# Prompt attention of a one-core decoder layer: the two heads of an output tile take turns, and values are weighed per query tile

## The chip, the core and the metric

The kernel runs on one core of a Trainium2 chip. The metric is the device time of one execution in microseconds (us). The engines are TensorE (PE, with its weight loads listed apart as PEld), VectorE (DVE), ScalarE (ACT), GpSimd (POOL) and SyncE (SP, which issues most DMAs). A name like L1465 is a line of the kernel file.

## What is computed

One layer over 512 prompt tokens and 8 sample tokens: a half-step feed-forward block, a mixer with 8 forgetting-attention heads (FoX) and 8 native-sparse-attention heads (NSA), and a second half-step feed-forward block. The change is in the mixer's attention over the prompt alone, cut here to that:

```python
# FoX, per head h, 64 dims, causal, 512 queries in blocks of 128
s = q @ k.T * scale + cum[q] - cum[k];  s = where(kpos <= qpos, s, NEG)
o_fox = softmax(s) @ v
# NSA, per head h (key/value head h // 4): selected and window branches, the same shape each
o = gate_slc * softmax(mask(q @ k_slc.T)) @ v_slc + gate_win * softmax(mask(q @ k_win.T)) @ v_win + compressed branch
```

With 512 tokens every block is selected and the window covers everything, so both NSA branches are plain causal attention.

## The kernel before, in words

The prompt's queries are cut into four tiles of 128 (i = 0 to 3); tile i looks at the keys 0 to 128(i+1). A unit is one head, one branch and one query tile. There are 96: 32 for FoX (8 heads by 4 tiles) and 64 for NSA (8 heads by 2 branches by 4 tiles). `unit(v)` (L128) numbers them: head by head, and inside a head (and branch) the tiles i = 0, 1, 2, 3. Four units with the same head and branch are a run; there are 24 runs.

A unit passes five steps, spread over the engines:

- `scores(v)` on TensorE (L1426): two matmuls of query against key (width 256, 256, 384, 512 for i = 0 to 3), for FoX one bf16 matmul with the forget sums (L1440), and one with the causal mask (L1442), all into a PSUM bank, of which FoX has four and NSA three.
- VectorE takes the row maximum (L1051), ScalarE the exponential with its sum (L756), VectorE the reciprocal (L1056). The scaling (L448) is on VectorE for i = 2 and 3 and on GpSimd for i = 0 and 1.
- `turn_p(w)` on TensorE (L1445): i+1 transposes of 128 by 128 (L1451) into PSUM bank 4 or 5.
- `turn_out` (L458) copies them to the buffer PTS (L464): VectorE for even units, ScalarE for odd ones.
- `weigh` on TensorE (L1455): the values VT times PTS, f32, into 64 of the 128 PSUM partitions of bank 6 or 7: partitions 0 to 63 for the even head of a tile of the output, 64 to 127 for the odd head. Before, one call `weigh(run, kb)` does a whole run's key block kb: one matmul, whose moving side is the queries from kb*128 to 512, so 512, 384, 256 and 128 columns for kb = 0 to 3.

Two heads make one output tile OT; `pair_out` (L744, ScalarE) copies a finished one out of PSUM (L746), and the next user of that bank waits for it. There are 8.

The order on each engine is written out by hand. In TensorE's `attention` (L1485) a step v issues scores(v), then turn_p(v-3), then from v = 8 after the stage's start one weigh of the list, so one key block at each step; what is left is issued at the end in a row. In NSA, from unit 52 to 83, each step also issues two matmuls of the compression windows (`windows`, L1471, L1479). ScalarE and VectorE each have a loop over the same v, with exp(v) and then the copy of v-3, and max(v), reciprocal and scale of v-1, and the copy of v-3.

An f32 matmul of the program shows as two records in the trace, each with a weight load of its own: the 96 calls of weigh are 192 records of L1465.

FoX attention stands between two parts of the input projection (L1308); NSA attention follows the second part. After NSA, SP waits for the last weigh before it loads more of the sample tokens' caches (L555), and GpSimd before it clears buffers (L1279).

Of the kernel before, what the change touches and what calls it, by code (L numbers as in the profile page):

```python
# [24 lines left out]
F32 = mybir.dt.float32  # L25
# [7 lines left out]
P = 128  # L33
D_MODEL, SEQ, DEC, PAST, PAGE = 1024, 512, 8, 256, 128
TOK = SEQ + DEC
HALF = TOK // 2
DH, HF, HN, HKV = 64, 8, 8, 2
# [5 lines left out]
QT = SEQ // P  # L43
# [81 lines left out]
    return sum(t in kinds for t in TILES[:j])  # L125


def unit(v):  # L128

    if v < 4 * HF:  # L130
        return True, v // 4, 0, v % 4, v // 4
    w = v - 4 * HF
    return False, w // 8, (w // 4) % 2, w % 4, HF + w // 4


def runs_of_pair(t):

    return range(2 * t, 2 * t + 2) if t < 4 else range(HF + 4 * (t - 4), HF + 4 * (t - 3))


class Step:
# [24 lines left out]
def layer_kernel(nc, I, O):  # L166
    with ExitStack() as ctx:
        made = {}

        def sem(name):  # L170
            if name not in made:
                made[name] = ctx.enter_context(nc.semaphore(name))
            return made[name]
# [78 lines left out]
        att = Region(a0, asize)  # L252
# [5 lines left out]
        v0 = att.at  # L258
        VT = att.put("VT", [P, QT, 512], F32)
        p0 = att.at  # L260
        PTS = att.put("PTS", [P, 2, QT, SEQ], F32)
        t0 = att.at
        TR = att.put("TR", [P, 4, TOK], F32)
        r0 = att.at
# [192 lines left out]

        def turn_out(eng, copy, w, name):  # L458

            _, _, _, i, run = unit(w)  # L460
            eng.wait_ge(sem("att_turned"), w + 1)
            if run >= 2:
                eng.wait_ge(sem("att_pv"), run - 1)
            copy(PTS[:, run % 2, 0:i + 1, P * i:P * i + P],  # L464
                 ps[:, 4 + w % 2, 0:P * (i + 1)].rearrange("p (a n) -> p a n", n=P)).then_inc(sem(name), 1)

        block = ctx.enter_context(nc.Block())
# [3 lines left out]
        def _(sp):  # L471
# [79 lines left out]
            for g in range(NPAGE):  # L551
                sp.dma_start(VF[g // 8][:, g % 8, :],
                             I["fox_v"][bass.ds(page[g], 1)].rearrange("a p n -> p (a n)")
                             ).then_inc(sem("vf_in"), 16)
            sp.wait_ge(sem("att_pv"), HF + 2 * HN)  # L555
            for name in sorted({stored_sem(j) for j in STORED}):
                sp.wait_ge(sem(name), max(stored_count(j) for j in STORED if stored_sem(j) == name))
            for g in range(NPAGE):
# [30 lines left out]
        def _(act):  # L589
# [152 lines left out]


            def pair_out(t):  # L744
                act.wait_ge(sem("att_pv"), runs_of_pair(t)[-1] + 1)
                nc.scalar.copy(OT[:, t, 0:SEQ], ps[:, 6 + t % 2, :]).then_inc(sem("att_out"), 1)  # L746

            def attention(u0, u1, pairs):
                pairs = list(pairs)
                for v in range(u0, u1 + 3):  # L750
                    if v < u1:
                        W = P * (unit(v)[3] + 1)
                        act.wait_ge(sem("att_max"), v + 1)
                        if v >= 4:
                            act.wait_ge(sem("att_turned"), v - 3)
                        nc.scalar.activation(PR[:, v % 4, 0:W], ps[:, score_bank(v), 0:W], ACT.Exp,  # L756
                                             bias=row_max[:, v:v + 1], accum_out=row_sum[:, v:v + 1]).then_inc(
                            sem("att_exp"), 1)
                    w = v - 3
                    if w >= u0 and w % 2:  # L760
                        turn_out(act, nc.scalar.copy, w, "att_odd_out")
                    if pairs and w > 4 * runs_of_pair(pairs[0])[-1] + 6:
                        pair_out(pairs.pop(0))
                for t in pairs:
                    pair_out(t)
# [456 lines left out]
        def _(pool):  # L1222
# [53 lines left out]
            nc.gpsimd.memset(QBN[:, :], 0.0).then_inc(sem("qb_cleared"), 1)  # L1276
            attention(4 * HF, 96)

            pool.wait_ge(sem("att_pv"), HF + 2 * HN)  # L1279
            nc.gpsimd.memset(KCS[:, :, :].bitcast(F32), 0.0).then_inc(sem("kc_cleared"), 1)  # L1280
            nc.gpsimd.memset(VCZ[:, :, :], 0.0).then_inc(sem("vc_cleared"), 1)
            nc.gpsimd.memset(PZ[0][:, :, :], 0.0).then_inc(sem("pz_cleared0"), 1)
# [12 lines left out]
        def _(pe):  # L1295
# [156 lines left out]
                                            PR[:, w % 4, kb * P:kb * P + P], ident)  # L1452
                q.then_inc(sem("att_turned"), 1)

            def weigh(run, kb):  # L1455

                fox, h, br, _, _ = unit(4 * run)
                t, j = (h // 2) + (0 if fox else 4), h % 2
                c = h * DH if fox else br * P + (h // 4) * DH
                if kb == 0:  # L1460
                    pe.wait_ge(sem("att_even_out"), 2 * run + 2)
                    pe.wait_ge(sem("att_odd_out"), 2 * run + 2)
                    if t >= 2 and j == 0 and br == 0:
                        pe.wait_ge(sem("att_out"), t - 1)
                q = nc.tensor.matmul(ps[64 * j:64 * j + 64, 6 + t % 2, kb * P:SEQ], VT[:, kb, c:c + DH],  # L1465
                                     PTS[:, run % 2, kb, kb * P:SEQ], start=kb == 0 and br == 0,
                                     stop=kb == QT - 1 and (fox or br == 1), skip_group_check=True)
                if kb == QT - 1:
                    q.then_inc(sem("att_pv"), 1)

            def windows(step):  # L1471

# [10 lines left out]
                        q.then_inc(sem("cmp_hid"), 1)  # L1483

            def attention(u0, u1):  # L1485
                parts = [(run, kb) for run in range(u0 // 4, u1 // 4) for kb in range(QT)]
                for v in range(u0, u1 + 3):
                    if v < u1:
                        scores(v)
                    if v - 3 >= u0:  # L1490
                        turn_p(v - 3)
                    if v >= 4 * parts[0][0] + 8:
                        weigh(*parts.pop(0))
                    if HID_FROM <= v < HID_FROM + 2 * CMP_LEN // HID_PER_UNIT:
                        windows(v - HID_FROM)
                for run, kb in parts:
                    weigh(run, kb)

            project(0, NB1)
            pe.wait_ge(sem("stack_lo"), of_kind(NB1, STACKED))  # L1500
# [275 lines left out]
```

## Time and profile before

| | |
|---|---|
| median of 3 runs | 1329.59 us (1329.27 to 1329.98) |
| span of the profiled execution | 1327.7 us |
| TensorE busy | 1259.9 us, 95% |
| VectorE, ScalarE, GpSimd busy | 569.3, 454.3, 174.6 us |
| FoX attention in the profile | about 507 to 563 us |
| NSA attention in the profile | about 631 to 768 us |

The profile is one execution. Its span, 1327.7 us, lies 1.9 us below the median of the timed runs; that much lies around the span. A row of a timeline gives start, duration, engine, line, operation, output<-input, the tile of the array (rows by columns), and how many records were merged. In brackets stands the engine's idle time before it and what ended it. Ends of matmuls are modelled and overlap, so the time from one start to the next says what an operation really takes, not its duration.

### The profile page before, as it was taken

What the parts mean: (1) busy time and instruction counts of PE and PEld (TensorE: products, weight loads), DVE (VectorE), ACT (ScalarE), POOL (GpSimd) and SP (SyncE); (2) the same over time, 40 slices, a digit from 0 to 9 for tenths busy, and PEclk for the clock granted to TensorE, in tenths of its full rate; (3) what the DMA queues carried; (4) which work ended last, traced back from release to release, by engine and by line L of the source; (5) the groups of instructions that cost most, each with busy time, mean ns of one, the idle gap of its engine ahead of it and who ended that gap; (6) DMA issues with size and microseconds to landing.
All of it is one profiled execution on the core that took longest, in us unless ns stands there. A gap on an engine that the chain in (4) does not pass through costs nothing.

```text
span 1327.7 us, 22995 instructions
## 1 busy us (share of the span) xinstructions
PE 1259.9 (95%) x9234; PEld 1121.9 (85%) x9234; DVE 569.3 (43%) x896; ACT 454.3 (34%) x767; POOL 174.6 (13%) x157
## 2 busy tenths in 40 slices
PE   8999999999998898999999988798999999999994
PEld 6999999999996895499566543596999999999993
DVE  4334333343337665456533542636433333343333
ACT  5222212222335635442533432345322221222342
POOL 0111100101114001122101100034011100001113
PEclk9999999999999999999999989899999999999997
DMA  6222233222231241011600544011122222322221
GB/s 254 96 95 95 72 96 111 80 88 83 80 123 41 74 144 48 1 64 65 211 0 0 193 117 137 32 65 64 64 95 95 79 87 95 109 79 92 80 80 65
DMA packets 46001, 117.91 MB, mean 89 GB/s; under 512 B 4154, under 2 KB 21818, under 8 KB 39874
## 3 DMA queue, kind: packets, MB, share of 16 engines
q1 hardware_dynamic: 42738, 110.95, 24.8%
q10 hardware_dynamic: 3184, 5.88, 1.2%
q8 instruction: 54, 0.88, 0.3%
q14 instruction: 25, 0.20, 0.0%
HBM read 110.93 MB, written 7.97 MB: 90 GB/s over the span
## 4 chain that ended last, share of the span: by engine, by line
PE 87%; DVE 5%; ACT 3%; issue 2%; DMA 1%; POOL 1%; POOLq 0%; ACTq 0%; SPq 0%; DVEq 0%
PE ps L1308 68%; PE ps L1465 5%; PE ps L1479 3%; PE ps L1436 3%; PE ps L1451 2%; DVE UT L890 1%; PE ps L1317 1%; PE ps L1599 1%; DVE XL L870 1%; POOL H L1252 1%; DVE QST L964 1%; ACT QST L674 1%; PE ps L1608 1%; DMA RAW<-in_w_gu 0%; PE ps L1401 0%
## 5 line engine op out<-in xcount | busy, mean ns | idle before, releaser
L1308 PE MATMUL ps<-XH,WH 128*128 128x260 f32 x1904 | 390.6, 286 | 20.0 <-DVE XL L870 13.7
L1308 PE MATMUL ps<-XH,WL 128*128 128x260 f32 x1904 | 384.6, 284 | 0.0
L1308 PE MATMUL ps<-XL,WH 128*128 128x260 f32 x1904 | 384.2, 283 | 0.0
L403 ACT CAST WH<-RAW 128x1024 fp32r<-128x1024 f32 (+2 forms) x183 | 174.8, 956 | 505.1 <-PE ps L1308 495.8
L1308 PEld LDWEIGHTS ps<-XH,WH 128*128 128x128 f32 x1904 | 295.7, 189 | 27.6 <-DVE XL L870 14.0
L1308 PEld LDWEIGHTS ps<-XH,WL 128*128 128x128 f32 x1904 | 294.5, 189 | 0.0
L1308 PEld LDWEIGHTS ps<-XL,WH 128*128 128x128 f32 x1904 | 294.0, 189 | 0.0
L406 DVE TENSOR_TENSOR WL<-RAW,WH 128x1024 fp32r<-128x1024 f32 (+2 forms) x183 | 203.5, 1112 | 154.8 <-ACT WH L403 153.6
L1308 PE MATMUL ps<-UL,WH 128*128 128x260 f32 x704 | 141.9, 283 | 0.0
L1308 PE MATMUL ps<-UH,WL 128*128 128x260 f32 x704 | 141.5, 282 | 0.0
L1308 PE MATMUL ps<-UH,WH 128*128 128x260 f32 x704 | 141.4, 282 | 0.0
L1242 POOL TENSOR_TENSOR UL<-HT,UH 128x520 f32 (+1 forms) x44 | 57.6, 1310 | 612.3 <-ACT UH L641 612.3
L1308 PEld LDWEIGHTS ps<-UH,WL 128*128 128x128 f32 x704 | 108.5, 188 | 0.0
L1308 PEld LDWEIGHTS ps<-UH,WH 128*128 128x128 f32 x704 | 108.4, 188 | 0.0
L1308 PEld LDWEIGHTS ps<-UL,WH 128*128 128x128 f32 x704 | 108.3, 188 | 0.0
L906 DVE TENSOR_TENSOR UT<-ps,token_rstd 128x520 f32<-128x520 f32 x44 | 30.8, 700 | 145.8 <-PE ps L1308 145.8
L1051 DVE TENSOR_REDUCE row_max<-ps 128x1 f32<-128x128 f32 (+1 forms) x96 | 46.9, 489 | 91.4 <-PE ps L1442 91.4
L902 DVE TENSOR_TENSOR GT<-ps,token_rstd 128x520 f32<-128x520 f32 x44 | 30.8, 699 | 128.2 <-PE ps L1308 119.8
L756 ACT ACTIVATE PR<-ps,row_max 128x128 f32<-128x128 f32 (+1 forms) x96 | 50.6, 527 | 95.7 <-DVE row_max L1051 95.0
L1465 PE MATMUL ps<-PTS,VT 128*64 128x512 f32 (+1 forms) x192 | 70.4, 456 | 0.0
L1436 PE MATMUL ps<-KST,QST 128*128 128x256 f32 (+1 forms) x192 | 61.4, 404 | 2.3 <-ACT v_new L709 1.0
L1436 PEld LDWEIGHTS ps<-KST,QST 128*128 128x128 f32 x192 | 33.1, 199 | 30.6 <-ACT PR L756 17.3
(229 smaller groups left out, 1056.5 us busy)
## 6 DMA issues: line engine op xcount, KB each, us to landing
RAW<-in_w_gu SPq DMA_DIRECT2D x44, 1024.0 KB, 4.8
RAW<-in_w_down SPq DMA_DIRECT2D x16, 768.0 KB, 4.6
RAW<-in_w_in SPq DMA_DIRECT2D x11, 1024.0 KB, 4.8
RAW<-in_w_down SPq DMA_DIRECT2D x16, 640.0 KB, 4.3
KF<-in_fox_k SPq DMA_DIRECT2D x16, 256.0 KB, 4.1
VF<-in_fox_v SPq DMA_DIRECT2D x16, 256.0 KB, 5.8
RAW<-in_w_out SPq DMA_DIRECT2D x4, 1024.0 KB, 5.0
H<-in_x SPq DMA_DIRECT2D x4, 520.0 KB, 7.4
```

What stands on the lines that cost most here:

```text
L403: nc.scalar.copy(WH[:, par, 0:width], RAW[:, slot, j, 0:width]).then_inc(w_hi, 1)
L406: nc.vector.tensor_tensor(WL[:, par, 0:width], RAW[:, slot, j, 0:width], WH[:, par, 0:width], ALU.subtract).then_inc(w_lo, 1)
L756: nc.scalar.activation(PR[:, v % 4, 0:W], ps[:, score_bank(v), 0:W], ACT.Exp, bias=row_max[:, v:v + 1], accum_out=row_sum[:, v:v + 1]).the ...
L902: nc.vector.tensor_tensor(two(GT[:, st.par, :]), halves(0), two(R1[:, :]), ALU.mult).then_inc(sem("evac"), 1)
L906: nc.vector.tensor_tensor(two(UT[:, st.par, :]), halves(1), two(R1[:, :]), ALU.mult).then_inc(sem("evac"), 1)
L1051: nc.vector.reduce_max(row_max[:, v:v + 1], ps[:, score_bank(v), 0:W], AX.X, negate=True).then_inc(sem("att_max"), 1)
L1242: nc.gpsimd.tensor_tensor(row(UL, st.m), HT[:, st.par, :], row(UH, st.m), ALU.subtract).then_inc(sem("hid_lo"), 1)
L1308: q = nc.tensor.matmul(ps[:, 2 * slot + half, 0:HALF], w[:, par, cols], x[:, kt0 + kt, half * HALF:(half + 1) * HALF], start=first and kt ...
L1436: nc.tensor.matmul(bank[:, 0:n], QST[:, h, part, i * P:i * P + P], KST[:, k, 0:n], start=part == 0, stop=False, skip_group_check=True)
L1451: q = nc.tensor.transpose(ps[:, 4 + w % 2, kb * P:kb * P + P], PR[:, w % 4, kb * P:kb * P + P], ident)
L1465: q = nc.tensor.matmul(ps[64 * j:64 * j + 64, 6 + t % 2, kb * P:SEQ], VT[:, kb, c:c + DH], PTS[:, run % 2, kb, kb * P:SEQ], start=kb == 0 ...
L1479: q = nc.tensor.matmul(ps[:, 3, 0:N_WIN], W1[n][:, j, :], view(X[n][:, :], j, [[CMP_STRIDE, N_WIN]]), start=j == 0, stop=j == CMP_LEN - 1)
```

## The change

- `unit(v)` counts differently: the two heads of an output tile alternate, so units come as tile 0 of both heads, tile 1 of both, and so on. In NSA branch follows branch as before, but inside a pair of heads.
- `weigh(n)` is called once for two units (every second step, at v - 6 = 2n) and does one query tile of both heads: for each key block kb up to i, head even and head odd one after the other, each 128 columns wide, into partitions 0 to 63 and 64 to 127 of the same bank.
- PTS becomes eight slots of one unit each, in place of two slots of one run each. The copies wait for `att_pv` per pair of units.
- `pair_out`, the waits of SP and GpSimd and the threshold in ScalarE's loop count pairs of units (48) in place of runs (24).

```diff
+PAIRS = 48
+PT_SLOTS = 8
 def unit(v):
     if v < 4 * HF:
-        return True, v // 4, 0, v % 4, v // 4
+        return True, 2 * (v // 8) + v % 2, 0, v // 2 % 4, v // 8
     w = v - 4 * HF
-    return False, w // 8, (w // 4) % 2, w % 4, HF + w // 4
+    return False, 2 * (w // 16) + w % 2, w // 8 % 2, w // 2 % 4, 4 + w // 16
-def runs_of_pair(t):
-    return range(2 * t, 2 * t + 2) if t < 4 else range(HF + 4 * (t - 4), HF + 4 * (t - 3))
+def pairs_until(t):
+    return 4 * (t + 1) if t < 4 else 16 + 8 * (t - 3)
...
-        PTS = att.put("PTS", [P, 2, QT, SEQ], F32)
+        PTS = att.put("PTS", [P, PT_SLOTS, QT, P], F32)
...
-            if run >= 2:
-                eng.wait_ge(sem("att_pv"), run - 1)
-            copy(PTS[:, run % 2, 0:i + 1, P * i:P * i + P],
+            if w >= PT_SLOTS:
+                eng.wait_ge(sem("att_pv"), (w - PT_SLOTS) // 2 + 1)
+            copy(PTS[:, w % PT_SLOTS, 0:i + 1, :],
...
-            def weigh(run, kb):
-                ...
-                q = nc.tensor.matmul(ps[64 * j:64 * j + 64, 6 + t % 2, kb * P:SEQ], VT[:, kb, c:c + DH],
-                                     PTS[:, run % 2, kb, kb * P:SEQ], start=kb == 0 and br == 0, ...)
+            def weigh(n):
+                pe.wait_ge(sem("att_even_out"), n + 1)
+                pe.wait_ge(sem("att_odd_out"), n + 1)
+                fox, _, br, i, t = unit(2 * n)
+                first = br == 0 and i == 0
+                if first and t >= 2:
+                    pe.wait_ge(sem("att_out"), t - 1)
+                for kb in range(i + 1):
+                    for j in (0, 1):
+                        h = unit(2 * n + j)[1]
+                        c = h * DH if fox else br * P + (h // 4) * DH
+                        q = nc.tensor.matmul(ps[64 * j:64 * j + 64, 6 + t % 2, i * P:i * P + P], VT[:, kb, c:c + DH],
+                                             PTS[:, (2 * n + j) % PT_SLOTS, kb, :], start=first and kb == 0, ...)
+                q.then_inc(sem("att_pv"), 1)
...
-                    if v >= 4 * parts[0][0] + 8:
-                        weigh(*parts.pop(0))
+                    if v % 2 == 0 and v - 6 >= u0:
+                        weigh((v - 6) // 2)
...
-                for run, kb in parts:
-                    weigh(run, kb)
+                weigh(u1 // 2 - 1)
```

## Rows read from the trace of the kernel before

**Rows 1.** The page: TensorE's share, and VectorE's, of the whole span.
```profile
PE 1259.9 (95%) x9234; PEld 1121.9 (85%) x9234; DVE 569.3 (43%) x896; ACT 454.3 (34%) x767; POOL 174.6 (13%) x157
```

**Rows 2.** The chain that ended last, 505 to 775 us, shares by line.
```profile
by line: PE ps L1465 23.9%; PE ps L1308 21.6%; PE ps L1479 15.1%; PE ps L1436 14.5%; PE ps L1451 9.9%; PE ps L1401 2.3%; issue 2.2%; PE ps L1442 2.2%; PE ps L1440 1.9%; DVE row_max L1051 1.0%; DVE VCZ L1097 0.6%; ACT L782 0.5%; ACT VT L707 
```

**Rows 3.** Busy time of each engine in one run of FoX, NSA, NSA with windows.
```profile
536.47:543.23 6.76, 6.76 (x36) 3.45 (x35) 3.73 (x13) 3.21 (x10) 1.53 (x2) 1.00 0.01 2
646.13:652.34 6.21, 6.21 (x31) 3.10 (x32) 3.87 (x13) 3.21 (x10) 1.00 (x2) 1.00 0.94 271
680.20:690.70 10.50, 10.50 (x47) 6.39 (x47) 3.91 (x13) 3.21 (x10) 1.00 (x2) 1.00 0.00 0
```

**Rows 4.** TensorE's timeline, FoX steps each with a weigh.
```profile
540.63 0.22 PE L1442 MATMUL ps<-causalb,identb 128*128 128x128 bf16 x1
540.68 0.61 PE L1451 MATMUL ps<-consts,PR 128*128 128x128 f32 x4
541.22 0.65 PE L1465 MATMUL ps<-PTS,VT 128*64 128x256 f32 x2
541.80 0.73 PE L1436 MATMUL ps<-KST,QST 128*128 128x512 f32 x2
...
542.65 0.28 PE L1451 MATMUL ps<-consts,PR 128*128 128x128 f32 x1
542.87 0.43 PE L1465 MATMUL ps<-PTS,VT 128*64 128x128 f32 x2
543.23 0.39 PE L1436 MATMUL ps<-KST,QST 128*128 128x256 f32 x1
```

**Rows 5.** The same timeline at the start of FoX, before the first weigh.
```profile
514.30 0.63 PE L1451 MATMUL ps<-consts,PR 128*128 128x128 f32 x4
514.68 0.71 PE L1436 MATMUL ps<-KST,QST 128*128 128x512 f32 x2
...
515.51 0.28 PE L1451 MATMUL ps<-consts,PR 128*128 128x128 f32 x1
515.55 0.48 PE L1436 MATMUL ps<-KST,QST 128*128 128x256 f32 x2
```

**Rows 6.** The weigh matmuls by form, 510 to 775 us: count, busy us, mean ns.
```profile
L1465 PE MATMUL ps<-PTS,VT 128*64 128x512 f32 x48 | 25.7, 617 | 0.0
L1465 PE MATMUL ps<-PTS,VT 128*64 128x128 f32 x48 | 10.2, 294 | 0.0
```

**Rows 7.** Sample tokens: 32 records, 128 columns, half array, back to back (chain; line L1608).
```profile
832.08 3.64 PE ps L1608 x32
...
L1608 PEld LDWEIGHTS ps<-VS,PZS x32: 133/137/138, 832.0 to 835.3; 128*64 128x64 f32 x32
L1608 PE MATMUL ps<-VS,PZS x32: 272/273/323, 832.0 to 835.4; 128*64 128x128 f32 x32
```

**Rows 8.** Timeline: two weight loads of one weigh; f32r matmuls of the projection.
```profile
541.22 0.19 PEld L1465 LDWEIGHTS ps<-PTS,VT 128*64 128x64 f32 x2 [0.17 <-issue]
...
612.21 0.40 PE L1308 MATMUL ps<-XL,WH 128*128 128x260 f32 x2
612.45 0.40 PE L1308 MATMUL ps<-XH,WL 128*128 128x260 f32 x2
```

**Rows 9.** VectorE by form, 510 to 775 us: maximum, reciprocal, scale and copy.
```profile
L1051 DVE TENSOR_REDUCE row_max<-ps 128x1 f32<-128x512 f32 x24 | 16.6, 691 | 33.7 <-PE ps L1442 33.7
L1056 DVE RECIPROCAL row_inv<-row_sum 128x1 f32<-128x1 f32 x95 | 14.6, 154 | 1.2 <-ACT PR L756 1.0
L1051 DVE TENSOR_REDUCE row_max<-ps 128x1 f32<-128x384 f32 x24 | 13.3, 555 | 26.1 <-PE ps L1442 26.1
L464 DVE COPY PTS<-ps 128x384 f32<-128x384 f32 x24 | 12.9, 539 | 0.0
...
L448 DVE TENSOR_SCALAR PR<-PR,row_inv,gates 128x512 f32<-128x512 f32 x16 | 8.7, 547 | 0.6
L448 DVE TENSOR_SCALAR PR<-PR,row_inv,gates 128x384 f32<-128x384 f32 x16 | 7.7, 479 | 0.6
...
L464 DVE COPY PTS<-ps 128x128 f32<-128x128 f32 x24 | 6.8, 283 | 0.0
L1051 DVE TENSOR_REDUCE row_max<-ps 128x1 f32<-128x128 f32 x23 | 6.5, 284 | 8.4 <-PE ps L1442 8.4
```

**Rows 10.** Timeline at the end of FoX.
```profile
559.96 3.17 PE L1465 MATMUL ps<-PTS,VT 128*64 128x256 f32 x12
560.07 0.58 ACT L464 COPY PTS<-ps 128x512 f32<-128x512 f32 x1 [1.70 <-PE ps L1451]
```

**Rows 11.** SP's issues of the window data, and the first matmuls that use them.
```profile
639.43 0.43 SPq L539 DMA_DIRECT2D XK<-out_nsa  x1
...
L1479 PE MATMUL ps<-XK,W1K x64: 449/450/522, 660.2 to 700.3; 128*128 128x161 f32 x64
```

More of the change, by code:

```diff
@@ L458, in turn_out @@
         def turn_out(eng, copy, w, name):
-            _, _, _, i, run = unit(w)
+            i = unit(w)[3]
             eng.wait_ge(sem("att_turned"), w + 1)
-            if run >= 2:
-                eng.wait_ge(sem("att_pv"), run - 1)
-            copy(PTS[:, run % 2, 0:i + 1, P * i:P * i + P],
+            if w >= PT_SLOTS:
+                eng.wait_ge(sem("att_pv"), (w - PT_SLOTS) // 2 + 1)
+            copy(PTS[:, w % PT_SLOTS, 0:i + 1, :],
                  ps[:, 4 + w % 2, 0:P * (i + 1)].rearrange("p (a n) -> p a n", n=P)).then_inc(sem(name), 1)
@@ L554, in _ @@
                              ).then_inc(sem("vf_in"), 16)
-            sp.wait_ge(sem("att_pv"), HF + 2 * HN)
+            sp.wait_ge(sem("att_pv"), PAIRS)
             for name in sorted({stored_sem(j) for j in STORED}):
@@ L744, in pair_out @@
             def pair_out(t):
-                act.wait_ge(sem("att_pv"), runs_of_pair(t)[-1] + 1)
+                act.wait_ge(sem("att_pv"), pairs_until(t))
                 nc.scalar.copy(OT[:, t, 0:SEQ], ps[:, 6 + t % 2, :]).then_inc(sem("att_out"), 1)
@@ L761, in attention @@
                         turn_out(act, nc.scalar.copy, w, "att_odd_out")
-                    if pairs and w > 4 * runs_of_pair(pairs[0])[-1] + 6:
+                    if pairs and w > 2 * pairs_until(pairs[0]) + 2:
                         pair_out(pairs.pop(0))
@@ L1277, in _ @@
             attention(4 * HF, 96)
-            pool.wait_ge(sem("att_pv"), HF + 2 * HN)
+            pool.wait_ge(sem("att_pv"), PAIRS)
             nc.gpsimd.memset(KCS[:, :, :].bitcast(F32), 0.0).then_inc(sem("kc_cleared"), 1)
@@ L1453, in turn_p @@
                 q.then_inc(sem("att_turned"), 1)
-            def weigh(run, kb):
[L1457 to L1464, printed above, removed]
-                q = nc.tensor.matmul(ps[64 * j:64 * j + 64, 6 + t % 2, kb * P:SEQ], VT[:, kb, c:c + DH],
[L1466 to L1469, printed above, removed]
+            def weigh(n):
[10 more added lines that the diff above has]
+                        q = nc.tensor.matmul(ps[64 * j:64 * j + 64, 6 + t % 2, i * P:i * P + P], VT[:, kb, c:c + DH],
+                                             PTS[:, (2 * n + j) % PT_SLOTS, kb, :], start=first and kb == 0,
+                                             stop=i == QT - 1 and kb == i and (fox or br == 1),
+                                             skip_group_check=True)
+                q.then_inc(sem("att_pv"), 1)
             def windows(step):
@@ L1485, in attention @@
             def attention(u0, u1):
-                parts = [(run, kb) for run in range(u0 // 4, u1 // 4) for kb in range(QT)]
                 for v in range(u0, u1 + 3):
```

## The prediction

> **What bounds the kernel now.** I read the page first: TensorE is busy for 95% of the span, VectorE for 43% [rows 1]. The chain of waits for the stretch of both attentions says the same in detail: almost all of its pieces are TensorE's, and the largest line is the weighing of the values, L1465, with 23.9% of 270 us, 64.5 us [rows 2]. The busy times of single runs show that no engine but TensorE is full: in a FoX run of four units TensorE works all of 6.76 us, VectorE 3.73, ScalarE 3.21, GpSimd 1.53; in an NSA run 6.21 against 3.87, 3.21 and 1.00; in an NSA run with the compression windows 10.50 against 3.91. The granted clock is 1.00 in all three, the level of 2.4 GHz [rows 3]. So whatever TensorE is spared here comes off the span, until VectorE is next.
>
> **What the weighing costs now.** Two records of 128 columns in a row without a change of form start 0.114 us apart (32 records in 3.64 us) [rows 7]; an f32 record takes two clocks a column (128 columns are 0.107 us at 2.4 GHz, the other 0.007 is the price of a short record). A run has 1280 columns in two records each, so 2560 times 2 clocks, 2.13 us; 24 runs take 51.2 us. (The means of the forms, 617 ns for 512 columns and 294 for 128, are longer, since ends are modelled and overlap [rows 6].) That leaves 13 of the chain's 64.5 us for something else. The timeline shows what. All other matmuls around it use the whole array (128*128), the weighing uses half the columns (128*64). From one transpose to the next scores it is 0.04 us with no weigh between [rows 5] and 0.58 us with one of 128 columns [rows 4]: 0.58 - 0.04 - 0.213 = 0.33 us more than its columns. With four transposes and 256 columns it is 1.12 against 0.38: 1.12 - 0.38 - 0.427 = 0.31 us. I take 0.32 us for going into the half-array form and out again.
>
> A rule of the Trainium skill bears on that: TensorEngine Tiling (Array Packing), section Tiling Modes, says that changing the tiling mode, not just the tile, drains the engine. The 0.31 and 0.33 us are this case's number for it.
>
> **Fewer blocks.** Before, each step from v = 8 has a weigh, 27 in FoX and 59 in NSA with the left-over ones in one block, 86 blocks. After, every second step has one: steps 6 to 34 in FoX, 15 blocks (the last two calls adjoin), and 31 in NSA, 46 blocks. 40 blocks fewer at 0.32 us: 12.8 us saved.
>
> **The matmuls themselves.** The columns stay: 10 matmuls of 128 columns per head and branch in place of 4 of up to 512, so 24 times 10, 240 matmuls, 480 records. If they run one after the other as in rows 7, they take 480 x 0.114 = 54.7 us, 3.5 us more than now (the records of 512 columns pay hardly any short-record price: the 12 left-over records with 1664 columns need 2.77 us of columns and are 3.17 long to their modelled end [rows 10]).
>
> But each pair now names two different halves of the array. No row of the trace before has matmuls of both halves side by side (at the end of FoX the other half waits for a copy), so this is unknown and I bound it. Upper end: no overlap, 54.7 us. Lower end: all overlap, 27.4 us. Which is nearer? A half-array record uses 64 columns; the other 64 stand idle. What could forbid a second record beside it are the shared paths. The load path doesn't: two loads of 64 columns take 0.19 us where one takes 0.135, so they are 0.055 us apart [rows 8], 480 of them 26.4 us. The moving side doesn't seem to: the projection's f32r records stream 260 columns in 0.12 us [rows 8], twice what an f32 record asks for. And loads of the same rows already go on beside a running matmul: loads of 0.137 us at a spacing of 0.114 [rows 7]. So I take overlap as the likelier case. The order is even, even, odd, odd in records (each matmul is two), and starts stay in order; then the second record of one half goes beside the first of the other, and a block of r records takes r/2 + 1 places rather than r/2. Eight units have four blocks, of 4, 8, 12 and 16 records, so 3 + 5 + 7 + 9 = 24 places in place of 40. Twelve such groups: 288 places at 0.114 us, 32.8 us. Against 51.2 us that saves 18.4 us.
>
> Statements of the Trainium skill speak to this, and the sum uses none. TensorEngine Tiling (Array Packing), sections Tiling Modes and Theoretical Speedup, says that different tiles can run loads and matmuls in parallel, with up to twice the throughput at 64 columns; by it the weighing would take about 27 us. The Trainium skill's TensorE: Matmul & The Clock Gate, Part 3, gives 2.38 times for three column tiles, but also says that a load overlaps a running matmul only when the row groups differ, and here both halves use all rows. By that last rule every load would be exposed, 480 x 0.055 = 26 us more; rows 7 speak against it, since their loads overlap.
>
> **What comes next once TensorE is faster.** With these savings eight units take 13.5 - 1.28 - 1.54 = 10.7 us in FoX, 12.4 - 2.8 = 9.6 in NSA and 18.2 with windows. VectorE has 7.5 us and 7.7 us of work for eight units [rows 3], plus 0.26: its copies are now of 128, 256, 384 and 512 columns in place of 128 and 384 twice (by rows 9 the step per 128 columns is 0.13 us, so 0.41 and 0.67 us for the two not shown). On average it has room. But the heavy units now come in fours (tiles 2, 2, 3, 3), all scaled by VectorE. I walked through that stretch by its order: from the scores of the second tile-2 unit until the last tile-3 unit may be turned VectorE has four maxima (384, 512, 512 and 128 columns: 0.56, 0.69, 0.69, 0.28), four reciprocals (0.62), four scales (twice 0.48, twice 0.55) and two copies (0.41, 0.54), 5.8 us [rows 9]. TensorE has in between five transposing calls (14 transposes of 0.107, 1.5 us), the scores of five units (two records of 256 to 512 columns at one clock a column and the mask: 1.8 us in NSA; with the forget sums 2.4 in FoX), two weighs of 3 and 5 places (0.9 us) with 0.64 for their forms, and 0.07 to 0.1 us a step besides (the step from 514.68 to 515.55 [rows 5] is that much longer than its columns): 5.3 us in NSA and 5.9 in FoX. So about 0.5 us of waiting per group in NSA without windows (units 32 to 51 and 84 to 95, four groups), 2 us, none in FoX and none under the windows. The bounds: 0, and 12 us, if a wait of 1.5 us comes in each of the eight groups without windows (then VectorE's chain, not TensorE, sets them).
>
> GpSimd's scales come in fours too, 3.1 us in FoX at most for eight units (twice 1.53 [rows 3]) out of 10.7; hidden. The waits added: copies wait for the weigh of eight units before, issued five steps earlier, hidden; the weigh waits for two copies made two steps earlier, hidden; if it were not, the next scores would be queued behind it. The window data land far ahead of need: the last is issued at 639.4, used first at 660.2 [rows 11], and that use moves forward by some 6 us. The ends of both stages: the last pair's heaviest units follow each other, so the last scale is late while TensorE has only one weigh left to cover it (before, five left-over ones followed): 0.5 us each, 1 us. At the starts the weighing begins two steps earlier, in a stretch with waits: no price.
>
> **The sum.** -12.8 - 18.4 + 2 + 1 = -28.2 us. The profiled execution goes from 1327.7 to 1299.5 us, and with the 1.9 us around it to 1301.4 us. The range of this case: 1293 (full overlap, no waits: -12.8 - 23.8) to 1311 (12 us of waits in place of 2).
>
> **The rivals.** First: the halves don't overlap; only the switches go. -12.8 + 3.5 = -9.3, 1320.3 us. For it: nothing in the trace has ever run two halves at once, and one sequencer feeds both in order. Against it: the arguments of the paths above. Its range is 1316 to 1326.
>
> Second: they overlap, but VectorE's chain sets both attentions outside the windows, and the gain there is lost for the most part; -12.8 - 18.4 + 15, 1313.4 us. Against it: 83% load at most.
>
> Third, the slower one: a change from one half to the other costs a drain as the change of form does. There are 1 + 3 + 5 + 7 = 16 such changes in a group, 192 in all. Half of 0.32 us each makes 30.7 us, so 1329.6 - 9.3 + 30.7 = 1351 us. It decides from 0.049 us per change on. For it: a change of form does drain (rows 4 and 5). Against it: the form stays 128*64, and the output partitions differ, so there is nothing to wait for.
>
> Fourth: the price of 0.32 us belongs to each matmul group's length or to the wait for copies, and isn't spared: then 0 to 3 us are lost or won, about 1330 us. For it, little: rows 4 and 5 differ in the weigh alone.
>
> **Chances.** Forecast (overlap, TensorE still the bound) 0.58; first rival 0.26; second 0.06; third 0.06; fourth 0.04. A measurement of this kernel tells 0.2%, 2.7 us, from no change. Faster: 0.58 + 0.26 + 0.06 = 0.90; same 0.04; slower 0.06. The range for 8 in 10 has to take in the first rival's centre and most of its spread and the forecast's: 1292 to 1325 us; above it lie the third and fourth and a little of the first, below it what a better start of the stages might add.
>
> **What would show it.** In the profile after: 480 records of L1465, all 128 columns; their starts in a block of 16 records some 0.06 us apart if they overlap, 0.11 if not, 0.2 or more if a change of half drains. A weigh's entry and exit still about 0.32 us, at half as many places. VectorE's waits before its maxima shrink from the 33.7 us shown for the widest form [rows 9]; TensorE would show waits for the scale (L448) ahead of transposes in NSA outside the windows, about 2 us. The FoX stage shrinks by about 10 us, NSA by 18. The prediction is wrong if the pairs are serial, if loads of the other half wait for the running matmul, or if TensorE waits for VectorE for more than some 5 us.

## The result

The changed kernel takes 1296.09 us (median of 4 runs, 1294.54 to 1297.29) against 1329.78 us before (1329.27 to 1330.54): ratio 0.9747, interval 0.9733 to 0.9761, 33.7 us less. The forecast was 1301.4 us, with 1292 to 1325 as its range.

The page of the changed kernel: the span, each engine's busy time (to set against [rows 1]), and the granted clock in 40 slices. The last line is the clock of the kernel before.

```profile
span 1293.2 us, 23595 instructions
...
PE 1226.7 (95%) x9522; PEld 1130.8 (87%) x9522; DVE 572.3 (44%) x896; ACT 451.6 (35%) x767; POOL 174.9 (14%) x157
...
PEclk9999999999998999999999999898999999999997
```

```profile
PEclk9999999999999999999999989899999999999997
```

TensorE is as full as before, with 288 records more and 33.2 us less of busy time; the others do what they did. The weighing by form, in the window of both attentions (count, busy us, mean ns), answers to [rows 6]; the chain's shares by line there answer to [rows 2].

```profile
L1471 PE MATMUL ps<-PTS,VT 128*64 128x128 f32 x480 | 36.7, 283 | 0.0
```

```profile
by line: PE ps L1312 25.3%; PE ps L1485 16.4%; PE ps L1440 14.1%; PE ps L1471 13.8%; PE ps L1455 11.4%; issue 3.9%; PE ps L1405 2.7%; PE ps L1446 2.6%; DVE row_max L1055 2.5%; PE ps L1444 2.1%; DVE PTS L468 0.9%; ACT PTS L468 0.6%; ACT L786
```

The weighing (now L1471) held 64.5 us of the chain before and holds 13.8% of 230 us, 32 us, now: 33 us are gone in this one line. Read from the starts of TensorE's first and last matmuls of each stage, FoX took 56.2 us and takes 44.1; the projection between takes 68.9 both times; NSA took 135.0 and takes 112.2; the rest of the kernel after it 560.0 and 560.6.

TensorE's timeline shows the blocks. A row's count is of records, two for each matmul; the start of the next row tells what a block really takes. FoX (first four rows) answers to [rows 4]; the last pairs are NSA under the windows.

```profile
531.17 1.09 PE L1471 MATMUL ps<-PTS,VT 128*64 128x128 f32 x16
532.20 0.62 PE L1440 MATMUL ps<-KST,QST 128*128 128x384 f32 x2
...
534.18 0.44 PE L1471 MATMUL ps<-PTS,VT 128*64 128x128 f32 x4
534.55 0.73 PE L1440 MATMUL ps<-KST,QST 128*128 128x512 f32 x2
...
669.62 0.66 PE L1471 MATMUL ps<-PTS,VT 128*64 128x128 f32 x8
670.21 1.34 PE L1485 MATMUL ps<-XK,W1K 128*128 128x161 f32 x4
...
674.07 0.88 PE L1471 MATMUL ps<-PTS,VT 128*64 128x128 f32 x12
674.88 1.34 PE L1485 MATMUL ps<-XK,W1K 128*128 128x161 f32 x4
```

Blocks of 4, 8, 12 and 16 records take 0.37, 0.59, 0.81 and 1.03 us to the next instruction: 0.0545 us a record and 0.15 us beside. About 0.05 us of the 0.15 lies between the first two starts of each half (0.16 us in place of 0.109), the rest at the way out of the form. That is half of what a record costs in [rows 7]: two halves of the array work side by side, without the one place that I had given up in each block. The records' own starts say the same: they come in pairs, one for each half, 6 ns apart, and after the first step each half starts a new one every 0.109 us. Two rows of the view of busy time in short stretches, of L1471 alone (length, busy, number of records running, granted clock), show two records from the first moment on.

```profile
541.44:541.60 0.16, 0.15 (x2) 1.00 0.00 0
541.60:541.71 0.11, 0.11 (x4) 1.00 0.00 0
```

### The profile page after: what moved, and what is told of

Same layout as the page of the kernel before. It is cut to its first block, busy times and chain, and to the rows that moved or that the text cites. A ratio compares the mean times of both kernels' runs of the same rounds, so it can differ in the third digit from the quotient of the medians.

```text
span 1293.2 us, 23595 instructions
## 1 busy us (share of the span) xinstructions
PE 1226.7 (95%) x9522; PEld 1130.8 (87%) x9522; DVE 572.3 (44%) x896; ACT 451.6 (35%) x767; POOL 174.9 (14%) x157
## 4 chain that ended last, share of the span: by engine, by line
PE 86%; DVE 6%; ACT 4%; issue 2%; DMA 1%; POOL 1%; POOLq 0%; ACTq 0%; SPq 0%; DVEq 0%
PE ps L1312 70%; PE ps L1485 3%; PE ps L1440 3%; PE ps L1471 2%; PE ps L1455 2%; PE ps L1321 1%; DVE UT L894 1%; PE ps L1603 1%; DVE XL L874 1%; POOL H L1256 1%; DVE QST L968 1%; ACT QST L678 1%; PE ps L1612 1%; PE ps L1405 0%; PE ps L1446 0%
## 5 line engine op out<-in xcount | busy, mean ns | idle before, releaser
L1246 POOL TENSOR_TENSOR UL<-HT,UH 128x520 f32 (+1 forms) x44 | 57.9, 1315 | 612.0 <-ACT UH L645 612.0
L760 ACT ACTIVATE PR<-ps,row_max 128x128 f32<-128x128 f32 (+3 forms) x96 | 50.7, 529 | 72.9 <-DVE row_max L1055 72.3
L1055 DVE TENSOR_REDUCE row_max<-ps 128x1 f32<-128x128 f32 (+3 forms) x96 | 46.8, 488 | 58.9 <-PE ps L1446 58.7
L1440 PE MATMUL ps<-KST,QST 128*128 128x256 f32 (+2 forms) x192 | 61.9, 408 | 2.0 <-ACT v_new L713 1.0
L645 ACT CAST UH<-HT 128x520 f32 (+1 forms) x44 | 27.6, 627 | 86.0 <-DVE HT L917 86.0
L1455 PE MATMUL ps<-consts,PR 128*128 128x128 f32 x240 | 43.6, 280 | 3.3 <-ACT PTS L468 2.9
```

Of the source, the lines that this page charges most:

```text
L645: nc.scalar.copy(row(UH, st.m), HT[:, st.par, :]).then_inc(sem("hid_hi"), 1)
L1055: nc.vector.reduce_max(row_max[:, v:v + 1], ps[:, score_bank(v), 0:W], AX.X, negate=True).then_inc(sem("att_max"), 1)
L1246: nc.gpsimd.tensor_tensor(row(UL, st.m), HT[:, st.par, :], row(UH, st.m), ALU.subtract).then_inc(sem("hid_lo"), 1)
L1440: nc.tensor.matmul(bank[:, 0:n], QST[:, h, part, i * P:i * P + P], KST[:, k, 0:n], start=part == 0, stop=False, skip_group_check=True)
L1455: q = nc.tensor.transpose(ps[:, 4 + w % 2, kb * P:kb * P + P], PR[:, w % 4, kb * P:kb * P + P], ident)
```

## The experiments

Times are medians; before is 1329.1 to 1329.3 us in these comparisons, and the changed kernel in its own run among them 1295.02 us. Where several numbers of one stage stand together, they are read from the same starts as above. The spread between executions of one kernel goes in part with the mean granted clock: the kernel with one half for both heads takes 1311.25 and 1311.4 us at 0.977, and 1308.6 and 1309.2 us at 0.979. The single steps of 1 to 3 us further down (two pairs, the copy first, the scale on GpSimd, and the last two together) have intervals that overlap the changed kernel's, 0.973 to 0.9756; that of two pairs with the copy first ends where the changed kernel's begins. One half, the heads in turn, one unit, the narrow matmuls and all three stand clear of it.

**One half for both heads.** In NSA both heads write one half.

```diff
-                        q = nc.tensor.matmul(ps[64 * j:64 * j + 64, ...
+                        half = j if fox else br
+                        q = nc.tensor.matmul(ps[64 * half:64 * half + 64, ...
...
```

> The changed kernel, but in the NSA stage both heads of a block write the same column half (partitions 0 to 63 in the first branch, 64 to 127 in the second), so the two heads' sums are mixed there; blocks, records (480 in all, 320 of them here) and order stay. Theory: the halves overlap, 0.055 us a record in pairs of halves against 0.114 in one half, so 320 x 0.059 = 18.9 us come back, less some 3 us of waits for copies that then vanish: 1312 to 1315 us. Rival: the gain is that of fewer changes of form and the halves add nothing: 1296 us, as the changed kernel.

Measured: 1310.22 us, ratio to before 0.9851 (0.9834 to 0.9867), 14.1 to 15.2 us slower than the changed kernel. FoX, which is not touched, takes 44.0 us as there; NSA takes 127.8 in place of 112.2. NSA blocks of the trace:

```profile
633.80 1.96 PE L1472 MATMUL ps<-PTS,VT 128*64 128x128 f32 x16
635.69 0.62 PE L1440 MATMUL ps<-KST,QST 128*128 128x384 f32 x2
...
637.30 0.65 PE L1472 MATMUL ps<-PTS,VT 128*64 128x128 f32 x4
637.88 0.73 PE L1440 MATMUL ps<-KST,QST 128*128 128x512 f32 x2
```

16 records take 1.89 us against 1.03, four take 0.58 against 0.37: 0.109 us a record with the same 0.15 beside. 320 x 0.0545 = 17.4 us; 15.6 us came back in the stage. Under the windows, where TensorE never waits, it is 7.8 us for 144 records, the full 0.0545 each; the 1.8 us that are missing all lie outside the windows, where TensorE waited before too. The rival is out: the overlap is real, and it hangs on the two heads' records naming different halves. I had 1312 to 1315 us, from 0.114 us for a record where it is 0.109.

**The heads in turn.** First all of the even head, then all of the odd.

```diff
-                for kb in range(i + 1):
-                    for j in (0, 1):
+                for j in (0, 1):
+                    for kb in range(i + 1):
```

> The changed kernel, but inside a block all key blocks of the even head come first and then all of the odd head, in place of alternating. If matmuls start strictly in the order of the program, each half runs alone, 0.114 us a record, and nearly the whole overlap is lost: 480 x 0.059 = 28 us less the one place where the halves meet in each of 48 blocks (2.6 us) and the waits that vanish: 1318 to 1322 us. Rival: TensorE holds records of both halves back and starts them out of order: 1296 us.

Measured: 1304.25 us, ratio 0.9806 (0.979 to 0.9822): neither of the two. Blocks of this trace, and then the number of records running in three successive stretches of the last of them:

```profile
640.27 0.44 PE L1471 MATMUL ps<-PTS,VT 128*64 128x128 f32 x4
640.64 0.73 PE L1440 MATMUL ps<-KST,QST 128*128 128x512 f32 x2
...
643.13 0.66 PE L1471 MATMUL ps<-PTS,VT 128*64 128x128 f32 x8
643.72 0.50 PE L1440 MATMUL ps<-KST,QST 128*128 128x256 f32 x2
...
645.52 1.15 PE L1471 MATMUL ps<-PTS,VT 128*64 128x128 f32 x12
646.60 0.50 PE L1440 MATMUL ps<-KST,QST 128*128 128x256 f32 x2
...
647.76 1.58 PE L1471 MATMUL ps<-PTS,VT 128*64 128x128 f32 x16
649.27 1.07 PE L1485 MATMUL ps<-XK,W1K 128*128 128x161 f32 x3
```

```profile
647.75:648.24 0.49, 0.48 (x4) 1.00 0.00 0
648.24:648.60 0.36, 0.36 (x9) 1.00 0.00 0
648.60:649.10 0.50, 0.50 (x10) 1.00 0.00 0
```

A block of 4 or 8 records loses nothing (0.37 and 0.59 us), one of 12 takes 1.08 in place of 0.81 and one of 16 takes 1.51 in place of 1.03. In strict order of the program the second head would begin after the first one's last record has begun, and 16 records would take about 15 x 0.109 + 0.15 = 1.8 us. In the records' starts the odd head begins 0.49 us into the block of 16, beside the fifth of the even head's eight, with three of them not begun; in the block of 12 it begins beside the third of six, again with three not begun. So in this trace TensorE went past three records that waited for their half, and no further. Per group of eight units the loss is 0.27 + 0.48 = 0.75 us, for twelve groups 9.0 us; 8.2 to 9.2 us were measured (1304.25 against 1296.09 and 1295.02).

The Trainium skill, TensorE: Matmul & The Clock Gate, Part 3, says that matmuls start and end strictly in order of the program. For records of different column halves this trace shows otherwise.

**Two and two.** Two key blocks of one head, then the same two of the other, four records each.

```diff
-                for kb in range(i + 1):
-                    for j in (0, 1):
+                for j, kb in [(j, kb) for a in range(0, i + 1, 2) for j in (0, 1) for kb in range(a, min(a + 2, i + 1))]:
```

> The changed kernel, but a block takes two key blocks of the even head, then the same two of the odd head, so four records of one half and four of the other in turn. If TensorE can begin the other half while up to three records of this half have not started (as the starts in the kernel with the heads in turn show), nothing is lost: 1296 us. If records start strictly in the order of the program, a block of 16 takes 1.4 us in place of 0.9 and the kernel some 12 us more: 1308 us.

Measured: 1296.19 us, ratio 0.9753 (0.9738 to 0.9768), against 0.9743 (0.973 to 0.9756) for the changed kernel beside it: no difference that can be told. Its blocks of 8 and 12 records take what they take in the changed kernel to within 0.01 us, and a block of 16 takes 0.05 us more, so the order costs at most 0.8 us in all. Three waiting records are passed, as read from the kernel before this one.

**The changed kernel again.**

> The changed kernel itself, run again beside the next three as their measure: 1295 to 1297 us.

Measured: 1295.02 us (1294.8 to 1297.62). It stood beside two and two (above), the copy first with the scale on GpSimd, and all three (below). Its FoX stage takes 43.4 us in the profile, where the first profile had 44.1, and the clock says why. The first row is the first profile's FoX, the second this one's; then follow, in the same order, the starts of NSA up to the first window matmul (the last columns are the granted clock, the DMA share and GB/s).

```profile
507.47:551.59 44.12, 42.86 (x369) 30.36 (x369) 30.86 (x96) 27.59 (x85) 12.15 (x16) 0.96 0.01 1
509.28:552.65 43.37, 41.30 (x364) 29.36 (x368) 30.86 (x96) 27.34 (x85) 12.08 (x16) 1.00 0.01 1
620.47:644.00 23.53, 22.45 (x185) 16.53 (x185) 17.60 (x58) 14.72 (x49) 5.71 (x12) 0.93 0.84 278
621.45:645.59 24.14, 23.51 (x185) 17.36 (x185) 17.79 (x58) 14.79 (x49) 5.69 (x12) 0.87 0.83 272
```

The granted clock of 0.96 is 3.4 us of the stage at the lower level of 1.2 GHz; without them FoX is 0.75 us shorter, and with some 3 us more of them (0.87 against 0.93) the start of NSA is 0.6 us longer. So stages of single profiles are good to about 0.7 us, and more of a claim than that rests on medians.

**One unit in a block.** The new order of units and tiles, but each head weighed at a step of its own: `weigh(m)` does unit m, one head, alone.

```diff
-                    if v % 2 == 0 and v - 6 >= u0:
-                        weigh((v - 6) // 2)
+                    if v - 6 >= u0:
+                        weigh(v - 6)
...
-                weigh(u1 // 2 - 1)
+                for m in (u1 - 3, u1 - 2, u1 - 1):
+                    weigh(m)
```

> The new order of units and the weighing per query tile, but a block at each step for one head alone (90 blocks in place of 46), so never two halves side by side. Theory: 44 more changes of form at 0.32 us, 14.1 us, and no overlap, 480 x 0.059 = 28.3 us: 1296 + 42 = 1338 us, slower than before by 8. Rival, the overlap is worth nothing: 1310 us. Rival, the change of form costs nothing: 1324 us.

Measured: 1328.41 us, ratio 0.9992 (0.9982 to 1.0001): no difference from before. So the new order and the weighing per tile bring nothing alone that shows in the medians; it is the pairing, with the overlap and 44 blocks fewer, that brings 32 to 33 us. In the stretch of the windows, where TensorE never waits, the forecast's prices hold: 82.82 us here, 68.95 in the changed kernel. Of the 13.87 us the columns account for 8.7 (152 records at 0.109 against 144 at 0.0545 in that stretch), which leaves 5.15 us for 16 blocks, 0.32 us each.

I had 42 us between this kernel and the changed one, and 33 were measured. 2 us of the miss are the 0.114 us a record for 0.109. Another 2 us are an oversight about this kernel: its last blocks of each stage adjoin, and there the two heads do meet. NSA's last block:

```profile
762.28 2.24 PE L1471 MATMUL ps<-PTS,VT 128*64 128x128 f32 x28
```

Less one record's 0.28 us, its last record starts 1.96 us after the first, where 28 records of one half would need 27 x 0.109 and 0.05, 3.0 us. In the starts, the second head begins 0.275 us into the block with three records of the first not begun. The block at the end of FoX is the same, so 2.1 us are saved in both.

That leaves 38.2 us by the prices, and the two profiles are 31.9 apart in the two stages. Most of the other 6.3 us can be read. TensorE's listed waits for scales and copies come to 8.5 us in the changed kernel (its largest rows stand under two pairs below) and to 3.9 in this one:

```profile
PEld ps L1455 <- POOL PR L452: 1.8, 5, 0.8
...
PEld ps L1471 <- ACT PTS L468: 0.8, 5, 0.2
PE ps L1455 <- POOL PR L452: 0.7, 2, 0.6
PE ps L1455 <- DVE PTS L468: 0.4, 2, 0.2
```

That is 4.6 us, and 1.3 us are the clock, which is 1.00 at both of this kernel's starts and 0.96 and 0.93 in the changed kernel's first profile.

Against the kernel before there is a third difference. With 4 blocks more and the same columns this one should take 2.4 us more in the two stages (1.3 for the blocks, 1.1 for short records), less the 2.1 at the ends, so 0.3 us more. In the profiles it takes 3.0 less (FoX 54.18 against 56.18, NSA 134.04 against 135.03). Some 0.7 us of that is again the clock in FoX, 0.97 in the profile of before and 1.00 here. In the medians it takes only 0.9 less (1328.41 against 1329.27). So the new order gains 1.2 us by the medians and 2.6 by the profiles, where I had put a loss of 1. FoX in the profile of before, then here:

```profile
507.63:563.81 56.18, 54.56 (x273) 28.61 (x273) 29.95 (x96) 28.66 (x85) 12.20 (x16) 0.97 0.00 1
507.52:561.70 54.18, 52.77 (x369) 36.93 (x369) 31.73 (x96) 27.79 (x85) 12.19 (x16) 1.00 0.00 1
```

**Narrow matmuls.** Most of the weighing reads half of a tile's queries.

```diff
+                        wide = P if br == 0 and kb == 0 else 64
-                        q = nc.tensor.matmul(..., i * P:i * P + P], VT[...], PTS[..., kb, :], ...
+                        q = nc.tensor.matmul(..., i * P:i * P + wide], VT[...], PTS[..., kb, 0:wide], ...
```

> The changed kernel, but the weighing matmuls take only the first 64 of a tile's 128 queries, except for the first key block of each tile in the first branch; the other queries are left out of these sums. 352 of the 480 records are 64 columns wide. If the weight loads set the spacing (0.055 us each), it stays at 0.055 us and the time at 1296 us. If the moving columns do (2 halves of 0.107 us), it falls to some 0.03 us and the time by up to 352 x 0.025 = 9 us, to 1287 us.

Measured: 1287.86 us, ratio 0.9683 (0.9667 to 0.9699), 7.2 to 8.2 us less than the changed kernel, and in the trace

```profile
639.60 0.69 PE L1472 MATMUL ps<-PTS,VT 128*64 128x64 f32 x16
640.21 1.34 PE L1486 MATMUL ps<-XK,W1K 128*128 128x161 f32 x4
```

16 records of 64 columns take 0.61 us, 0.029 a record after the 0.15. So the moving columns set the 0.0545 us, not the weight loads, although each record still has its load of 64 columns. In [rows 8] two loads lay 0.055 us apart; those were of one half. In the changed kernel the loads of the two halves start 7 ns apart, so that spacing doesn't hold from one half to the other, and the lower end that I drew from the row, 26.4 us, wasn't one. What the halves share and what each has to itself isn't shown beyond this.

**Two pairs in a block.** Half as many changes of form again.

```diff
-                    if v % 2 == 0 and v - 6 >= u0:
-                        weigh((v - 6) // 2)
+                    if v % 4 == 0 and v - 8 >= u0:
+                        weigh((v - 8) // 2)
+                        weigh((v - 6) // 2)
...
+                weigh(u1 // 2 - 2)
                 weigh(u1 // 2 - 1)
```

> The changed kernel, but the weighing of two pairs of units stands in one block every fourth step: 24 blocks in place of 46, the same records. Theory: each change of form into the half-array matmuls and out costs TensorE 0.32 us, so 15 blocks fewer in FoX and under the windows bring 4.8 us and the 7 in the rest of NSA little or nothing, because waits for VectorE and ScalarE take them up: 1289 to 1292 us. Rival, the price hangs on the columns and not on the change: 1296 us. Rival, later weighing makes the copies wait: above 1296 us.

Measured: 1293.80 us, ratio 0.974 (0.9727 to 0.9753): hardly to be told from the changed kernel, and above the 1289 to 1292 us that I expected. Under the windows it holds: 68.95 us become 65.67, 3.28 less, of which 0.65 is a block of 12 records that falls out of the stretch and 2.6 is 8 blocks at 0.33 us. A block of 28 records runs on at the same pace, 1.68 us, which is 28 x 0.0545 and the 0.15:

```profile
677.94 1.75 PE L1471 MATMUL ps<-PTS,VT 128*64 128x128 f32 x28
679.62 1.34 PE L1485 MATMUL ps<-XV,W1V 128*128 128x161 f32 x4
```

Outside the windows nothing comes off (FoX 44.4 us against 43.4 to 44.1, the first 20 units of NSA 24.3 against 23.5): who waited for whom between 505 and 740 us, in total, times and longest, shows why. The first fence is the changed kernel, the second this one.

```profile
PEld ps L1455 <- DVE PR L452: 3.5, 6, 1.1
...
PE ps L1455 <- ACT PTS L468: 2.9, 5, 0.9
...
PEld ps L1455 <- POOL PR L452: 0.4, 2, 0.3
```

```profile
PE ps L1455 <- ACT PTS L468: 9.4, 15, 1.1
...
PEld ps L1455 <- DVE PR L452: 7.5, 8, 1.4
...
PEld ps L1455 <- POOL PR L452: 5.6, 10, 0.8
```

The transposes (L1455) wait for ScalarE's copy, which frees their PSUM bank, and for the scale by VectorE or GpSimd. Three steps without a weigh follow each long block, and the waits in them take the gain away.

**ScalarE's copy first.** In ScalarE's loop the copy of unit v - 3 comes ahead of the exponential of unit v.

```diff
                 for v in range(u0, u1 + 3):
+                    w = v - 3
+                    if w >= u0 and w % 2:
+                        turn_out(act, nc.scalar.copy, w, "att_odd_out")
                     if v < u1:
                         ...
-                    w = v - 3
-                    if w >= u0 and w % 2:
-                        turn_out(act, nc.scalar.copy, w, "att_odd_out")
```

> The changed kernel, but ScalarE's loop does the copy of unit v - 3 before the exponential of unit v. If TensorE's waits before transposes come from the order of ScalarE's queue (copy behind an exponential behind a maximum), 2 to 3 us go: 1293 to 1294 us. Rival, VectorE's lateness sets them: no change, 1296 us, or slower since exponentials start later.

Measured: 1293.40 us, ratio 0.973 (0.9717 to 0.9744), in the range expected. The wait for ScalarE's copy is gone from the list, and a smaller one for VectorE's copy stands in its place:

```profile
PEld ps L1455 <- DVE PR L452: 2.5, 4, 0.9
...
PE ps L1455 <- DVE PTS L468: 1.9, 5, 0.7
```

**Both.** Two pairs in a block and the copy first.

> Two pairs in one block and ScalarE's copy first, both at once. If the two causes are separate the gains add: 1286 to 1290 us. If the fewer blocks only turn into more waits, it is where the better of the two is, 1290 to 1293 us.

Measured: 1291.19 us, ratio 0.9716 (0.9703 to 0.973). That is 3.8 to 4.9 us less than the changed kernel, where two pairs alone took off 1.2 to 2.3 and the copy alone 1.6 to 2.7: what one would see if the gains add. By the ranges that I had set it falls into the second case, 1290 to 1293 us, and differences of this size aren't clear enough of the spread to choose.

**The scale on GpSimd.** In NSA tile 2 is scaled by GpSimd, so that VectorE scales tile 3 alone.

```diff
+        def dve_from(u):
+            return DVE_SCALES + (0 if unit(u)[0] else 1)
...
-                        if unit(u)[3] >= DVE_SCALES:
+                        if unit(u)[3] >= dve_from(u):
                             scale_p(dve, nc.vector.tensor_scalar, u)
...
-                    if unit(u)[3] < DVE_SCALES:
+                    if unit(u)[3] < dve_from(u):
                         scale_p(pool, nc.gpsimd.tensor_scalar, u)
```

> The changed kernel, but in NSA the scaling of tile 2 moves from VectorE to GpSimd. If VectorE's load over the heavy tiles makes TensorE's waits in NSA outside the windows (the trace shows some 3 us), it falls to 1293 us. Rival: the waits are ScalarE's, whose copy stands behind an exponential that waits for a maximum, and GpSimd's slower scale adds its own: 1296 us or above.

Measured: 1292.39 us, ratio 0.9723 (0.9708 to 0.9738). NSA takes 110.9 in place of 112.2 us, of it 18.7 in place of 19.7 after the windows, and under the windows 68.95 in both. That fits VectorE's lateness over the heavy tiles being part of what TensorE waits for, as forecast.

**The copy first and the scale on GpSimd.** The last two edits together, without the long blocks.

> The changed kernel with ScalarE's copy first and the scaling of NSA's tile 2 on GpSimd. Each takes away part of TensorE's waits in NSA outside the windows, which were 3 us in all, so together they can't bring more than those and 0.5 us in FoX: 1291 to 1293 us.

Measured: 1293.08 us, ratio 0.9724 (0.9711 to 0.9738), and 1.9 us less than the changed kernel beside it; its interval overlaps that one's by little. It is no faster than either edit alone (1293.40 and 1292.39): as if, with short blocks, the two took away the same waits, but that wasn't taken apart.

**All three.** Two pairs in a block, the copy first and the scale on GpSimd.

> All three: two pairs in one block, ScalarE's copy first, NSA's tile 2 scaled on GpSimd. With two pairs in a block the steps between blocks are short, and TensorE waits for scales of VectorE and GpSimd. If VectorE is the one that is late, this is the fastest, 1288 to 1290 us; if GpSimd is, it is no better than without its extra scale, 1291 us or above.

Measured: 1287.27 us (1286.86 to 1288.27), ratio 0.9686 (0.9672 to 0.9699), 41.9 us less than before and 7.8 less than the changed kernel beside it. It is the fastest version here, 0.7 us below what I had expected. The scale on GpSimd is worth 3.9 us on top of the other two, where on top of the copy alone it was worth less than 1. Its waits are short ones for GpSimd:

```profile
PEld ps L1458 <- POOL PR L452: 4.6, 13, 0.8
...
PEld ps L1458 <- DVE PR L452: 1.4, 3, 0.6
```

## Why the prediction was right, and which of its terms were not

The mechanism held: TensorE bounds both stages, the halves overlap, and a change of form costs 0.32 us. Of the first forecast's terms, each set against what the runs gave:

- **Fewer blocks: 12.8 us. Held.** The price came out of the windows' stretch of two kernels, 0.32 and 0.33 us a block; 40 blocks fewer are 13.0 us.
- **The matmuls: 18.4 us saved. Mis-sized; it is 25.0.** The steps that failed are the two corrections. I let starts be strictly in order and so gave each block one place more; the kernel with the heads in turn shows that TensorE passes up to three waiting records, so a block of r records takes r/2 places. And I took 0.114 us for a record of one half, the mean over 32 in [rows 7] with its way out; it is 0.109. 51.2 - 480 x 0.0545 = 25.0 us, close to the full overlap that I had named as the lower end. The choice of overlap over no overlap was right, though one of its reasons, the load path, was drawn from a row of one half and bore on something else.
- **The starts and ends of the stages: a loss of 1 us. Wrong in sign.** The kernel with one unit a block gains 1.2 to 2.6 us against the one before. The tiles now come light first, while the pipeline fills, and the weighing begins two steps earlier, in time in which TensorE waited; these are the candidates, and they were not taken apart.
- **The waits for VectorE: 2 us. Too small.** 13.0 + 25.0 = 38.0 us and the gain of the order, 1.2 to 2.6, should have come off the two stages, and 34.9 did (12.1 and 22.9), so 4.3 to 5.7 us are waits and clock. That is a difference of sums; beside it stand the listed waits for scales and copies, 3.9 us with one unit a block and 8.5 in the changed kernel, and 0.6 us of clock at the start of NSA (0.93, before 1.00). Before, the same list came to 7.2 us, so against that kernel the waits rose by 1.3 us alone. I had walked through VectorE's work alone, whose scales are the largest row (3.5 us). Missing was ScalarE's copy (2.9 us), which stood behind an exponential that waited for VectorE's maximum; I had called the copies hidden, since they come two steps before they are needed by the weigh, and overlooked that the next transposes need their bank two units later. The listed waits for VectorE alone, 3.5 for scales and 1.7 for copies, are just above the 5 us that I had named as a sign of being wrong.
- **Nothing elsewhere.** The projection took 68.9 us both times, the rest 0.6 us more. That the loads were never late I take from there being no wait for the window data in TensorE's list.

The forecast was short by 6.3 us in the profiled span and 5.3 in the median, and that is the overlap: 6.6 us for the matmuls, with 0.6 of the rest of the kernel against it. The two small terms were each wrong and came out right together by luck: I had put a loss of 1 us for the order and 2 for waits, 3 in all, and 38.0 - 34.9 = 3.1 us were lost, a gain of 1.2 to 2.6 by the order and 4.3 to 5.7 of waits and clock.

**The rivals.** No overlap: out, by one half for both heads. VectorE as the bound: out, since both stages fell by 34.9 us where this rival had 16; it costs a few us, and scaling one tile elsewhere gave 2.6 to 3.7 us, not clear of the spread. A drain at each change of half: out, a block of 16 records changes halves seven times and goes on at 0.0545 us a record. The price of 0.32 us not saved: out, by the stretch under the windows.

What I said would show it did: 480 records of 128 columns, spacing 0.055, entry and exit the same at half the places. FoX shrank by 12 us and NSA by 23, where I had 10 and 18. And VectorE's waits before its widest maxima went down from 33.7 to 6.0 us:

```profile
L1055 DVE TENSOR_REDUCE row_max<-ps 128x1 f32<-128x512 f32 x24 | 16.5, 686 | 6.0 <-PE ps L1446 6.0
```

## What to carry to other kernels

Where TensorE is the bound, matmuls whose outputs take 64 partitions or fewer belong in pairs, one for each column half of the array, next to each other: here the pairing was worth 32 us, and the same matmuls unpaired nothing. Longer blocks between full-width matmuls save another 0.32 us for each way in and out, in blocks of 2 to 28 records alike, but only where the other engines keep up: alone, twice as long blocks brought 1 to 2 us of the 7 that they spared. When TensorE gets faster, look at once at who hands it its next inputs and frees its banks: a queue in fixed order, with a copy behind an instruction that waits, made a third of TensorE's listed waits, and moving that copy and one tile's scale made the long blocks pay, 7.8 us in all.

## What the runs showed of the hardware that I had not expected

- Records of the two column halves overlap fully, in f32: 0.0545 us a record of 128 columns against 0.109 in one half, and 0.029 for 64 columns.
- TensorE starts a record of the other half while three of this half have not begun, and was never seen to pass a fourth (one half after the other, blocks of 8 records cost nothing, of 12 cost 0.27 us, of 16 cost 0.48; in turns of four records a block of 16 costs 0.05).
- Loads of the two halves start 7 ns apart, where two of one half are 0.055 us apart in [rows 8], and 16 records of 64 columns with a load each all start within 0.46 us.
